# Products of a constant by itself in TensorE's waits between output projection and experts

## What is computed

```
x = x + memory_cross_attention(rms_norm(x, norm_cross), rms_norm(mem, norm_mem), ...)   # ends in  o @ wo
x = x + hierarchical_moe(rms_norm(x, norm_ffn), wg, bg, we, be, w_gate, w_up, w_down)

def hierarchical_moe(xn, ...):
    g_prob = softmax(xf @ wg + bg);  g_idx = argmax(g_prob)            # 4 groups
    e_logits = xf @ we + be                                            # 32 experts, 8 in a group
    top_v, top_i = top_k(the 8 logits of the chosen group, 2)
    weights = g_prob[g_idx] * softmax(top_v)
    tokens sorted by expert;  y = (silu(xs @ w_gate) * (xs @ w_up)) @ w_down * weights
    out = sum of y over each token's two experts
```

## Time and profile before

| | us |
|---|---|
| median of 3 runs | 2089.68 |
| lowest and highest of them | 2087.22 and 2089.76 |
| the profiled execution's own time | 2087.57 |
| its span, first to last instruction | 2085.8 |

### The profile page before, as it was taken

The page is one execution under the profiler, slowest core; times in us unless marked ns, Lnnn a source line. Parts: engine busy times, 40 slices in busy tenths (PEclk is TensorE's granted clock), DMA queues, the critical chain, the costliest instruction groups (busy, mean ns, idle before and its releaser), DMA issues.

```text
span 2085.8 us, 22869 instructions
## 1 busy us (share of the span) xinstructions
PE 1935.5 (93%) x9584; PEld 1229.0 (59%) x9584; DVE 784.8 (38%) x1130; ACT 509.7 (24%) x880; POOL 114.0 (5%) x134
## 2 busy tenths in 40 slices
PE   7999989886999999999799969989878999999997
PEld 5874767575444444443488869977565444444443
DVE  4466474335222232222333363455352322322222
ACT  3417253422101101100244332335231011011010
POOL 2200010001000000000100050100010000000000
PEclk9999999997999999999899999999988999999999
DMA  6220333032999999999434202432024999999996
GB/s 224 81 81 1 122 131 101 21 104 79 393 413 412 407 413 408 410 408 412 164 101 142 99 19 85 132 101 81 27 98 187 419 411 405 411 409 411 409 408 277
DMA packets 100186, 491.12 MB, mean 235 GB/s; under 512 B 7777, under 2 KB 16017, under 8 KB 50801
## 3 DMA queue, kind: packets, MB, share of 16 engines
q1 hardware_dynamic: 96928, 478.18, 58.4%
q0 software_dynamic: 2576, 9.33, 1.3%
q10 hardware_dynamic: 576, 2.10, 0.3%
HBM read 487.48 MB, written 2.10 MB: 235 GB/s over the span
## 4 chain that ended last, share of the span: by engine, by line
PE 86%; DVE 7%; ACT 4%; issue 2%; POOL 1%; DMA 0%; DVEq 0%; ACTq 0%; POOLq 0%
PE ps L615 24%; PE ps L899 22%; PE ps L914 11%; PE ps L869 7%; PE ps L891 6%; PE ps L612 6%; PE ps L854 2%; PE ps L847 1%; PE ps L645 1%; PE ps L628 1%; DVE wl L498 1%; PE ps L760 1%; PE ps L883 1%; PE ps L906 1%; DVE al L1539 1%
## 5 line engine op out<-in xcount | busy, mean ns | idle before, releaser
L899 PE MATMUL ps<-ring,xg 128*64 128x512 f32 x1536 | 346.3, 596 | 0.0
L498 DVE TENSOR_TENSOR wl<-ring,wh 128x512 fp32r<-128x512 f32 x280 | 191.7, 695 | 398.7 <-ACT wh L489 397.4
L489 ACT ACTIVATE wh<-ring 128x512 fp32r<-128x512 f32 x280 | 174.2, 629 | 445.3 <-PE ps L615 367.9
L1939 DVE TENSOR_TENSOR x<-ps,x 128x1024 f32<-128x1024 f32 x128 | 150.6, 1219 | 335.2 <-PE ps L891 335.2
L615 PE MATMUL ps<-wh,ah 128*128 128x512 f32 x544 | 216.7, 398 | 10.0 <-DVE al L1601 4.7
L899 PEld LDWEIGHTS ps<-ring,xg 128*64 128x64 f32 x1536 | 104.8, 137 | 198.7 <-issue 194.7
L615 PE MATMUL ps<-wl,ah 128*128 128x512 f32 x544 | 214.7, 395 | 0.0
L615 PE MATMUL ps<-wh,al 128*128 128x512 f32 x544 | 214.4, 394 | 0.0
L914 PE MATMUL ps<-ring,hT 128*64 128x512 f32 x768 | 173.5, 601 | 1.4 <-ACT hT L1381 1.4
L869 PE MATMUL ps<-oh,xnh 128*128 128x256 f32 x512 | 133.6, 298 | 5.2 <-DVE oh L1957 5.2
L869 PEld LDWEIGHTS ps<-oh,xnh 128*128 128x128 f32 x512 | 99.2, 194 | 52.5 <-issue 52.5
(11 more groups left out here) (280 smaller groups left out, 2570.4 us busy)
## 6 DMA issues: line engine op xcount, KB each, us to landing
ring<-in_moe_w_gate SPq DMA_DIRECT2D x96, 1024.0 KB, 9.2
ring<-in_moe_w_up SPq DMA_DIRECT2D x96, 1024.0 KB, 8.4
ring<-in_moe_w_down SPq DMA_DIRECT2D x96, 1024.0 KB, 8.4
slot<-in_moe_w_up SPq DMA_DIRECT2D x32, 1024.0 KB, 8.9
slot<-in_moe_w_gate SPq DMA_DIRECT2D x32, 1024.0 KB, 9.3
slot<-in_moe_w_down SPq DMA_DIRECT2D x32, 1024.0 KB, 9.0
ring<-in_x_wkv SPq DMA_DIRECT2D x16, 1024.0 KB, 5.1
ring<-in_c_w_in SPq DMA_DIRECT2D x16, 1024.0 KB, 5.3
```

Of the source, the lines that this page charges most:

```text
L489: act.activation(wh[:, t % STAGE, :], ring[:, unit % RING, 512 * s:512 * (s + 1)], ACT.Copy).then_inc(wh_ready, 1)
L498: dve.tensor_tensor(wl[:, t % STAGE, :], ring[:, unit % RING, 512 * s:512 * (s + 1)], wh[:, t % STAGE, :].bitcast(F32), ALU.subtract).then ...
L899: mm = pe.matmul(ps[p * SLOTS:(p + 1) * SLOTS, bank, :], xg[:, b % 2, k, r * P + p * SLOTS:r * P + (p + 1) * SLOTS], w(p)[:, k % 4, :], st ...
L1939: return dve.tensor_tensor(x[:, m, :], ps[:, bank:bank + 2, :].rearrange("p a n -> p (a n)"), x[:, m, :], ALU.add)
```

## The change

A helper issues n products of `identr` by `identr`, spread to 512 columns, into a given bank. Nobody reads them and they signal nothing. They are put on TensorE's queue at seven places in each layer: 16, 6, 6 and 6 in the four rounds of the norm before the experts, after `begin` and before the wait for `nat_ready`, into bank b+2 of the round's half; 6 after the fourth tile's transposes, ahead of `split_written`; 20 after `begin` of the rank round, ahead of the wait for `cnt_ready`; 8 after the rank's products, ahead of the experts. Other norms pass no `idle` and stay as they are.

```diff
+            def idle_products(bank, n):
+
+                for _ in range(n):
+                    pe.matmul(ps[:, bank, :].rearrange("p (a n) -> p a n", n=P), identr[:, :],
+                              identr[:, :].unsqueeze(1).to_broadcast([P, TM, P]), start=True, stop=True)
+
-            def norm_T(kind, l, tiles):
+            def norm_T(kind, l, tiles, idle=()):
 
                 for m in tiles:
                     b = begin((kind, l, m))
+                    if idle:
+                        idle_products(b + 2, idle[m])
                     nats[0] += 1
                     pe.wait_ge(nat_ready, nats[0])
...
-                norm_T("nffn", l, range(TM))
+                norm_T("nffn", l, range(TM), (16, 6, 6, 6))
+                idle_products(4 * HALF["nffn", l, TM - 1] + 2, 6)
                 split_written("nffn", l, TM)
                 thin("route", l, l + 1)
...
                 b = begin(("rank", l, 0))
+                idle_products(b + 2, 20)
                 pe.wait_ge(S["cnt_ready"], l + 1)
...
                 mm.then_inc(acc_done, 1)
+                idle_products(b + 2, 8)
                 experts(l)
```

## The result

The changed kernel took 2076.57 us in the median of six runs (2073.72 to 2079.82) against 2089.70 for the kernel before in the same runs: a ratio of 0.9941, 95% interval 0.9931 to 0.9951. The profiled execution took 2075.24 us, its span is 2073.5, its mean granted clock 0.976 instead of 0.964.

The account below looks back on a forecast made before the run. TensorE holds most of the chain; between projection and experts VectorE binds, with TensorE partly on the path at half clock. Gains of 5.95 and 6.4 us, less 1.2, give 11.2: 2076.4 us, 2078.5 at the median's level; range 2074.9 to 2085.

Parts of the forecast that it names:

- the 12.35 of the sum: Both layers' gains between output projection and experts if the clock holds: 5.95 and 6.4 us, together 12.35 us.
- 1.2 had been taken off: Deduction of 1.2 us from the summed gain, for one clock fall somewhere: a quicker transpose tile or two thirds of a rank.
- rival 3: Added products don't count for the clock; TensorE at 1.2 GHz overruns its waits: 15.9 us slower, 2105.6 us, chance 0.06.
- Norm: Norm before the experts: transposes of tiles 0 and 3 at full clock win 0.3 and 0.9 us, 1.2 us per layer.
- at full clock the products cost nothing; that cover is VectorE's chain: In the filled waits, added products at full clock hide behind VectorE's work and add 0 us; at half clock they don't.
- fitted their waits: Batches end within TensorE's waits, leaving 1.55 us before tile 0, 1.7 and 0.85 us before the two layers' ranks.
- Router: Router's 24 products take 5.7 us at full pitch instead of 7.53 and 7.62 us: gain 1.8 and 1.9 us.
- gather: Gather's 48 products: about 13.5 and 17.5 cold ones gain 0.09 us each, 1.25 and 1.6 us.
- Rank: Rank's 16 fp32 products, cold in 3.57 us, gain 1.7 us in both layers, estimated from the transposes' ratio.
- rival 1: Clock holds in part, falling at longer waits before tile 0 or layer 0's rank: gain 6 to 10 us, 2082, chance 0.27.
- Does the clock hold: Step on whether filled waits keep full clock: 1.55 and 1.7 us waits stay; one fall somewhere costs 1.2 us.
- Rival 2: Clock falls in the norm, isn't back before the router, which starts 4.3 us late per layer: 2092 us, chance 0.10.

Follow-up runs that it names:

- half-size run: Against the changed kernel, half of each batch: 8, 3, 3, 3, 3, 10 and 4 products; 2082.06 us, ratio 0.9971.

## Why the prediction was right, and where its terms were off

The forecast was 11.2 us won, the measured median 13.1 in one series of runs and 9.2 in the other; the stages account for 10.2. That the total came so near is in part luck: the stages gave 2.2 us less than the 12.35 of the sum, where 1.2 had been taken off, and the rest of the run moved by up to 3 us for reasons that the forecast doesn't have. The mechanism is shown: the granted clock is 1.00 where it was 0.50, the stages behind each batch shorten, the batches work one by one, and twice as many give 2091.88 us by overrunning, as rival 3 has it for products at half clock. Rival 3 itself, that products of a nearly empty constant don't count, is refuted: with them the clock is 1.00 through the norm and the router, and without the sixes it falls there. By its steps:

**Norm, 1.2 us each forecast, 0.63 measured.** The transposes did what was said, but the step "at full clock the products cost nothing; that cover is VectorE's chain" was wrong: the cover itself got longer. Kernel after, layer 0 (start, duration, engine, line):

```profile
469.78 1.09 PE L636 MATMUL ps<-ident,xn 128*128 128x128 f32 x8 [1.54 <-DVE xn L1526]
470.63 1.64 PE L624 MATMUL ps<-identr 128*128 128x512 f32 x6
472.76 1.22 DVE L1550 TENSOR_TENSOR al<-ps,ah 128x1024 fp32r<-128x1024 f32 x1
479.55 1.09 PE L636 MATMUL ps<-ident,xn 128*128 128x128 f32 x8 [0.54 <-DVE xn L1526]
```

VectorE goes from a scaling to a subtraction and on without a pause until the last low part, as forecast, and three scalings took 0.26, 0.20 and 0.23 us longer than 2.07. With one column as moving operand the gain was 1.36 us, a little over the forecast. The batches fitted their waits as worked out: 1.54 us left before tile 0 (1.55 forecast), 1.7 to 1.8 and 0.8 us before the ranks (1.7 and 0.85).

**Router, 1.8 and 1.9 forecast, 1.70 and 1.80 measured; gather, 1.25 and 1.6 forecast, 1.39 and 1.66 measured.** The chain's pieces of the kernel after, answering to the earlier trace rows:

```profile
483.06 5.83 PE ps L653 x24
...
502.04 5.75 PE ps L877 x48
...
1548.30 5.82 PE ps L653 x24
...
1565.52 5.98 PE ps L877 x48
```

**Rank, 1.7 forecast; 1.52 measured in layer 1, 0.83 in layer 0.** The 16 products take 1.97 us warm (1560.78 to 1562.75), close to the 1.9 estimated from the transposes. In layer 1 something else is then late, in the chain of the kernel after:

```profile
1562.51 0.42 DVE tab L1921
1562.93 0.02 issue
1562.95 0.30 DVE rt L1923
```

VectorE, which waited 1.67 us for the rank before, now comes to it from its own table work, just after the products have ended. The forecast didn't name that limit. In layer 0 the fall that was taken off came where it was expected, and cost 0.7 us, where the forecast took 1.2 off and rival 1 has 1.7: it came when most of the rank was done. Its second half is overrun. The eight products at half clock end after the selection matrix is ready:

```profile
497.63 1.26 PE ps L1109 x8
498.89 3.15 PE ps L624 x8
```

The matrix was done at 500.08 + 1.22 = 501.30 us and the gather's first product started at 501.87.

**Does the clock hold.** The step was right in its doubt and in its sum: one fall in two layers. A wait of 1.5 to 1.6 us before tile 0, with products up to its start and dense transposes and products behind it, held in both layers of every profile with all sixteen. The rule of the Trainium skill (TensorE: Matmul & The Clock Gate, Part 4: PE-mode transpose), that transposes don't count as busy, is not borne out as it stands, since transposes alone had raised the clock; but without any products between them they didn't keep it up here, and three products a tile did. The same page's section "A second HAM failure mode: psum-queue depth-cycling" has a kernel whose frequent short pauses between groups of products make the clock swing. No run here tests that: layer 0's rank and the run that leaves the eight out show one fall each, behind waits of 1.78 us and of 2.63 and 2.78 us, and not a swing.

**Rival 2** did not happen: with its six products a tile the clock never fell in the norm. Its step that a clock fallen there isn't back before the router is spoken against by the half-size run: with three products a tile cold work fills the norm so well that the clock came back 3.4 us later, and the early fall cost next to nothing. What a fall costs with six was not run.

What stays open: up to 3 us by which the totals differ from the sum of the stages, in one direction in the one series and in the other in the other. Part of it goes with where other falls land. One such fall lies in the last pair of experts, from 2051 to 2055 us in the profile after and not in that of before. From layer 1's first expert product to its last down projection (L922 in the kernel after) it is 486.9 us in the three profiles with a fall there (the two of the change and the one of twice each batch) and 485.2 in the ten others. No run held those falls fixed.

## What to carry to other kernels

If TensorE's work behind a wait is on the path, look at its granted clock before its length; work that nobody reads, put into the wait, can return what the lower clock costs there, here 1.7 to 1.8 us of a router of 7.1 to 7.2. What runs beyond the wait delays the stage behind it: twice each batch lost the whole gain. Start from stages that are seen to be on the path: 33 us more at full clock in other waits moved the median by 2 us. Let the filler read as little as it can, for instance one column spread out.

## What the runs showed of the hardware that was not expected

- Products with a 128x128 moving operand read four times slow VectorE's strided scaling beside them, from 2.07 us to between 2.25 and 2.33 in the kernel after; with a single column read 512 times it stays at 2.05 to 2.08. VectorE's subtractions from PSUM aren't touched: in the run with twice each batch they ran beside such products for their whole length and took 1.23 us, as before.
- The clock can fall while TensorE is at work: 1.4 us into layer 0's rank after a wait of 1.78 us, and 0.9 us into layer 0's gather where the wait of 2.63 us behind the rank was left empty.
- Nothing in the added products changes, and the operand is nearly all zeros; the clock is held all the same, at 1.00 through the norm and the router of both layers.
- In the kernel before, a VectorE operation of the routing took 1.08 us instead of 0.29 beside a GpSimd operation of 1.10 us, and with that layer 0's wait before the rank is 0.8 us longer.
